# Router logits taken from raw rows and scaled after, expert rows gated on the way out of PSUM, last expert turn written out with column halves

## The reference, cut to what matters

```python
x = x + g_m * y                                     # end of the mixer
h = rms_norm(x, norm_ffn[l]) * (1.0 + sc_f) + sh_f  # 256 rows of 1024
logits = h @ w_router                               # 1024 -> 8
top_val, top_idx = lax.top_k(logits, 2)
top_w = jax.nn.softmax(top_val, -1)
for e in range(8):
    out = out + combine[..., e:e+1] * (silu(h @ w1[e]) * (h @ w3[e])) @ w2[e]
x = x + g_f * out
```

## Time and profile before

| what | value |
|---|---|
| median of 3 runs | 2612.45 us (2610.32 to 2614.62) |
| the profiled execution's own time | 2612.26 us |
| its span, first to last instruction | 2610.5 us |
| mean granted TensorE clock | 0.972 of 2.4 GHz |
| busy: PE, PEld, DVE, ACT | 2460.1, 1437.8, 614.0, 455.7 us |
| read from HBM | 583.14 MB |
| issue of the first expert load | 1676.29 us |

### The profile page before, as it was taken

How to read it: one execution, slowest core, us unless ns; L and a number is a source line. 1 busy time by engine, 2 the same in 40 slices (tenths; PEclk the granted TensorE clock), 3 DMA queues, 4 the chain that set the end, 5 groups by cost and what they waited for, 6 DMA issues and landing times.

```text
span 2610.5 us, 36347 instructions
## 1 busy us (share of the span) xinstructions
PE 2460.1 (94%) x15945; PEld 1437.8 (55%) x15945; DVE 614.0 (24%) x1457; ACT 455.7 (17%) x949; POOL 48.2 (2%) x67
## 2 busy tenths in 40 slices
PE   7999999999999999999999999799999889989987
PEld 5754776756685547777677655444443334333333
DVE  1241556713444320000144332300000001001001
ACT  1321123322213310000122142200010000001000
POOL 3300000000000000000000000000000000000000
PEclk9999899998999999999999999799999999999999
DMA  8633633327224137434532521399999999999995
GB/s 255 127 129 105 233 133 137 129 105 258 67 99 161 65 111 276 151 140 175 190 89 98 194 93 37 112 393 394 394 393 394 393 394 394 391 396 388 389 393 212
DMA packets 258237, 586.58 MB, mean 225 GB/s; under 512 B 14592, under 2 KB 16720, under 8 KB 258080
## 3 DMA queue, kind: packets, MB, share of 16 engines
q1 hardware_dynamic: 254304, 576.93, 60.2%
q0 software_dynamic: 3376, 5.94, 1.4%
q10 hardware_dynamic: 400, 1.36, 0.2%
HBM read 583.14 MB, written 1.06 MB: 224 GB/s over the span
## 4 chain that ended last, share of the span: by engine, by line
PE 84%; DMA 8%; SPq 3%; DVE 2%; ACT 1%; issue 1%; DVEq 1%; ACTq 0%
PE PSA L325 15%; PE PSB L2555 12%; PE PSA L340 10%; PE PSB L2489 7%; DMA RING<-in_w_moe 7%; PE PSA L2584 5%; PE PSA L2471 4%; PE PSB L2568 4%; PE PSA L699 3%; SPq L2847 3%; PE PSA L1278 2%; PE PSA L1901 2%; PE PSA L2594 2%; PE PSB L1470 1%; PE PSA L1852 1%
## 5 line engine op out<-in xcount | busy, mean ns | idle before, releaser
L2555 PE MATMUL PSB<-RING,Y 128*64 128x512 f32 x1792 | 399.9, 599 | 41.1 <-issue 20.8
L325 PE MATMUL PSA<-RING,HT 128*128 128x512 f32 (+1 forms) x896 | 392.5, 587 | 8.6 <-ACT Y L1441 5.0
L340 PE MATMUL PSA<-HT,RING 128*128 128x256 f32 x1216 | 277.8, 389 | 8.6 <-DMA RING<-in_w_in_ab 4.2
L2555 PEld LDWEIGHTS PSB<-RING,Y 128*64 128x64 f32 x1792 | 133.2, 138 | 270.4 <-issue 258.0
L325 PEld LDWEIGHTS PSA<-RING,HT 128*128 128x128 f32 x896 | 165.7, 191 | 183.2 <-issue 178.0
L340 PEld LDWEIGHTS PSA<-HT,RING 128*128 128x128 f32 x1216 | 235.0, 195 | 45.1 <-issue 11.7
L2584 PE MATMUL PSA<-RING,ROW 128*64 128x512 f32 x896 | 198.4, 595 | 5.6 <-issue 4.3
L2489 PE MATMUL PSB<-HT,RING 128*128 128x256 f32 x896 | 199.8, 381 | 2.0 <-DMA RING<-in_w_dense 2.0
L2489 PEld LDWEIGHTS PSB<-HT,RING 128*128 128x128 f32 x896 | 171.2, 191 | 37.2 <-issue 12.4
L2682 DVE TENSOR_TENSOR ROW<-ROW,PSB 128x512 f32<-128x512 f32 (+2 forms) x56 | 28.2, 504 | 589.7 <-PE PSB L2555 553.0
L2568 PE MATMUL PSB<-RING,Y 128*32 128x128 f32 (+1 forms) x3136 | 132.9, 289 | 0.0
(11 more groups left out here) (444 smaller groups left out, 2256.8 us busy)
## 6 DMA issues: line engine op xcount, KB each, us to landing
RING<-in_w_moe SPq DMA_DIRECT2D x168, 2048.0 KB, 20.1
RING<-in_w_ada SPq DMA_DIRECT2D x24, 2048.0 KB, 8.1
RING<-in_w_dense SPq DMA_DIRECT2D x21, 2048.0 KB, 11.9
RING<-in_w_in SPq DMA_DIRECT2D x20, 2048.0 KB, 11.6
RING<-in_w_in_c SPq DMA_DIRECT2D x15, 2048.0 KB, 8.0
RING<-in_w_in_ab SPq DMA_DIRECT2D x10, 2048.0 KB, 15.6
RING<-in_w_out SPq DMA_DIRECT2D x4, 2048.0 KB, 7.8
RING<-in_w_out_ab SPq DMA_DIRECT2D x3, 2048.0 KB, 7.8
```

Source lines behind the costliest of these rows:

```text
L325: mm = pe.matmul(PSA[:, lane[k], 512 * t:512 * t + cols], HT[:, c, P * t:P * t + P], W[:, c, 0:cols], start=(c == 0), stop=(c == KC - 1))
L340: mm = pe.matmul(PSA[:, lane[k], S * j:S * j + S], W[:, c, P * j:P * j + P], HT[:, c, :], start=(c == 0), stop=(c == KC - 1))
L2555: mm = pe.matmul((UP if up else GATE)[WIDE * which:WIDE * which + WIDE, :], HTG[:, c, WIDE * which:WIDE * which + WIDE], W[which][:, c, :] ...
```

## The change

- At the end of layer 1's mixer VectorE first runs `dve_moe_prepare`: scale, shift and gate of the second half of `mod`, `router_w` multiplied by the scale, the shift's product with the router's weights, the spreading of the gate, four memsets. Tile t=1 of the gated add is done in two column halves, each with its own `x_ready`.
- `pe_entry`, `act_entry`, `dve_entry` are not called for the experts. `pe_router` turns the raw rows of X (transposes), t=0 ahead of t=1; ScalarE copies three half tiles to HT and VectorE the fourth; the logits are `raw * rms + shift`, formed by VectorE after the root.
- `dve_router` goes through both tiles one after the other, signals `chosen`, and forms the rank as soon as the counts are there (two matmuls, ahead of the places); places, the first selection, weights and the count of turns come after `ranked`, in that order. The gate row is spread by eight matmuls behind the places. The phases "ffn", "experts done" and "ffn done" of layer 1 are gone; the slot numbers in the constants count from 1, which saves an offset.
- VectorE multiplies both OUT tiles by GATE_ROW as they go to YG; ACC starts as a copy of X (made in g=1 of turn 0).
- The loop runs over turns 1 and 2 and the last turn is written out, without its gathers. Its last two loads are four, by column halves, with two semaphores of their own; `down` of the last group runs half by half, as do the products with the gate, the scatters (order 0, 2, 1, 3), the adds and the store (four of 256 KB).
- In the first block some semaphores are merged, and GpSimd drains after its first memset instead of signalling `padded`.

The diff, cut to its core:

```diff
+            if l == 1:
+                dve_moe_prepare(dve)
             for t in range(NT):
...
-                dve.tensor_tensor(MIXED[:, t, :], PSA[:, t, :], GATE_ROW, ALU.mult)
-                dve.drain()
-                dve.tensor_tensor(X[:, t, :], X[:, t, :], MIXED[:, t, :], ALU.add).then_inc(sem("x_ready"), 1)
+                for cols in [slice(0, 512), slice(512, 1024)] if l and t else [slice(0, 1024)]:
+                    dve.tensor_tensor(MIXED[:, t, cols], PSA[:, t, cols], GATE_ROW[:, cols], ALU.mult)
+                    dve.drain()
+                    dve.tensor_tensor(X[:, t, cols], X[:, t, cols], MIXED[:, t, cols], ALU.add).then_inc(sem("x_ready"), 1)
...
         def pe_router(pe):
+            need(pe, "gate_spread")
+            for t in range(NT):
+                for hf in range(2):
+                    if t == 0 and hf == 0 or t == 1:
+                        need(pe, "x_ready")
+                    for c in range(4):
+                        mm = pe.transpose(PSB[:, 2 * t + hf, P * c:P * c + P], X[:, t, 512 * hf + P * c:512 * hf + P * c + P], ident)
+                    mm.then_inc(sem("h_turned"), 1)
+                if t == 0:
+                    pe.matmul(PSA[:, 0, N_EXP:2 * N_EXP], CF[:, C_ONE:C_ONE + P], router_shift, start=True, stop=True)
+                for c in range(KC):
...
+                    mm = pe.matmul(PSA[:, 0, 512 * t:512 * t + N_EXP], HT[:, c, P * t:P * t + P], router_w[:, c, :],
+                                   start=(c == 0), stop=(c == KC - 1))
+                mm.then_inc(sem("logits"), 1)
+            need(pe, "chosen")
+            for t in range(NT):
+                mm = pe.matmul(COUNTS, CF[:, C_ONE:C_ONE + P], chosen[:, t, :], start=(t == 0), stop=(t == NT - 1))
+            mm.then_inc(sem("places"), 1)
...
+            for c in range(KC):
+                mm = pe.matmul(PSB[:, c // 4, P * (c % 4):P * (c % 4) + P], SPREAD[:, c, :], ident, start=True, stop=True)
+            mm.then_inc(sem("gate_row"), 1)
...
         def act_router(act):
+            for t in range(NT):
+                need(act, "x_ready")
+                if t:
+                    need(act, "x_ready")
+                act.activation(H2[:, t, :], X[:, t, :], ACT.Square, accum_out=rms_x[:, t:t + 1])
+                if t:
+                    act.drain().then_inc(sem("x_squared"), 1)
+                for hf in range(2 - t):
+                    act.wait_ge(sem("h_turned"), H_TURNED + 2 * t + hf + 1)
+                    act.activation(HT[:, 4 * hf:4 * hf + 4, P * t:P * t + P], PSB[:, 2 * t + hf, :].rearrange("p (c q) -> p c q", c=4),
+                                   ACT.Copy).then_inc(sem("h_taken"), 1)
+            act_rs(act, rms_x)
...
         def dve_router(dve):
+            need(dve, "x_squared")
+            k = dve_rs_ask(dve, rms_x, 1.0 / D, EPS)
+            dve.wait_ge(sem("h_turned"), H_TURNED + 4)
+            dve.tensor_copy(HT[:, 4:8, P:2 * P], PSB[:, 3, :].rearrange("p (c q) -> p c q", c=4)).then_inc(sem("h_taken_late"), 1)
+            dve.wait_ge(sem("rs_done"), k)
+            for t in range(NT):
+                need(dve, "logits")
...
+                dve.scalar_tensor_tensor(logits[:, t, :], PSA[:, 0, 512 * t:512 * t + N_EXP], rms_x[:, t:t + 1], router_shift,
+                                         ALU.mult, ALU.add)
...
+            dve.drain().then_inc(sem("chosen"), 1)
+            dve.tensor_tensor(top_w[:, :, 1], top8[:, :, 1], top8[:, :, 0], ALU.subtract)
+            dve.drain().then_inc(sem("act_input"), 1)
+            need(dve, "places")
+            dve.scalar_tensor_tensor(rank_key, COUNTS, float(N_EXP), place, ALU.mult, ALU.subtract)
+            dve.drain()
+            dve.max(rank_sorted, rank_key)
+            dve.drain()
+            dve.max_index(rank_i.bitcast(U32), rank_sorted, rank_key)
+            dve.drain().then_inc(sem("ranked"), 1)
...
+            for hf in range(2):
+                pe.wait_ge(sem(f"last_columns{hf}"), 32)
+                down_wide(GROUPS - 1, (512 * hf,), False)
+                down_extra(GROUPS - 1, (512 * hf,)).then_inc(sem("last_rows"), 1)
+            pe.wait_ge(sem("misc_free"), pieces(turn, SCATTERS + 1))
+            for piece in LAST_PIECES:
+                pe.wait_ge(sem("moe_rows"), turn + (piece % 2 + 1))
+                scatter_piece(pe, piece, piece).then_inc(sem("last_rows"), 1)
...
-            act.wait_ge(sem("item_used"), used(turn, (0, "down", GROUPS - 1)))
-            act.activation(YG[0], OUT[0], ACT.Copy).then_inc(sem("moe_rows"), 1)
...
-            dve.tensor_copy(YG[1], OUT[1]).then_inc(sem("moe_rows"), 1)
...
+            if not end:
+                dve.wait_ge(sem("item_used"), used(turn, (0, "down", GROUPS - 1)))
+                for k in range(2):
+                    e = dve.tensor_tensor(YG[k], OUT[k], GATE_ROW, ALU.mult)
+                e.then_inc(sem("moe_rows"), 1)
+                return
+            for hf in range(2):
+                cols = slice(512 * hf, 512 * hf + 512)
+                need(dve, "last_rows")
+                for k in range(2):
+                    e = dve.tensor_tensor(YG[k][:, cols], OUT[k][:, cols], GATE_ROW[:, cols], ALU.mult)
+                e.then_inc(sem("moe_rows"), 1)
+            for piece in LAST_PIECES:
+                need(dve, "last_rows")
+                dve_add(dve, piece, piece).then_inc(sem("result"), 1)
...
+            for hf in range(2):
+                for j in (PER_TURN - 2, PER_TURN - 1):
...
+                    if hf == 0:
+                        sp.wait_ge(sem("item_used"), last * PER_TURN + (STATIC + j - SLOTS + 1))
+                    sp.dma_start(slot_view(j)[:, :, cols], src).then_inc(sem(f"last_columns{hf}"), 16)
```

More of the change, by code:

```diff
@@ L2325, in dve_router @@
-            for t in range(NT):
-                dve.tensor_scalar(chosen1, place, top8[:, t, 0:1], None, ALU.is_equal)
-                dve.drain()
-                dve.scalar_tensor_tensor(chosen[:, t, :], place, top8[:, t, 1:2], chosen1, ALU.is_equal, ALU.add)
+                dve.drain()
+                dve.tensor_copy(top_f[:, t, :], top_i[:, t, :].bitcast(U32))
+                dve.drain()
+                dve.tensor_scalar(chosen1, place, top_f[:, t, 0:1], None, ALU.is_equal)
+                dve.drain()
@@ L2329, in dve_router @@
+                dve.scalar_tensor_tensor(chosen[:, t, :], place, top_f[:, t, 1:2], chosen1, ALU.is_equal, ALU.add)
                 dve.drain()
             dve.drain().then_inc(sem("chosen"), 1)
-            need(dve, "top_exp")
+            dve.tensor_tensor(top_w[:, :, 1], top8[:, :, 1], top8[:, :, 0], ALU.subtract)
+            dve.drain().then_inc(sem("act_input"), 1)
+            need(dve, "places")
+            dve.scalar_tensor_tensor(rank_key, COUNTS, float(N_EXP), place, ALU.mult, ALU.subtract)
@@ new lines, in dve_router @@
+            dve.drain()
+            dve.max(rank_sorted, rank_key)
+            dve.drain()
+            dve.max_index(rank_i.bitcast(U32), rank_sorted, rank_key)
+            dve.drain().then_inc(sem("ranked"), 1)
+            dve.tensor_copy(rank_f, rank_i.bitcast(U32))
+            need(dve, "places")
+            for t in range(NT):
+                dve.scalar_tensor_tensor(e_place[:, t, :], PLACES[:, 8 * t:8 * t + 8], 1.0, chosen[:, t, :], ALU.add, ALU.mult)
+            dve.drain()
+            dve.tensor_tensor(PERMUTE, place.unsqueeze(1).broadcast_to([P, N_EXP, N_EXP]),
+                              rank_f.unsqueeze(2).broadcast_to([P, N_EXP, N_EXP]), ALU.is_equal)
@@ new lines, in dve_router, with by_rank @@
+            dve.drain()
+            halves = [slice(0, 4), slice(7, 3, -1)]
+            def by_rank(to, src):
+                for t in range(NT):
+                    dve.tensor_tensor(PERMUTED[:, t, :, :], PERMUTE, src[:, t, :].unsqueeze(1).broadcast_to([P, N_EXP, N_EXP]), ALU.mult)
+                dve.drain()
+                for which in range(2):
+                    dve.tensor_reduce(to[which][:, :, 0:4], PERMUTED[:, :, halves[which], :], AX.X, ALU.add)
+                dve.drain()
+            by_rank(t_place, e_place)
@@ L2332, in dve_router @@
+            dve_select(dve, 0)
+            dve.drain().then_inc(sem("select"), 1)
+            need(dve, "act_output")
             dve.tensor_scalar(top_w[:, :, 0], top_w[:, :, 1], 1.0, None, ALU.add)
@@ L2336, in dve_router @@
             dve.tensor_tensor(top_w[:, :, 1], top_w[:, :, 1], top_w[:, :, 0], ALU.mult)
-            for k in range(2):
-                dve.memset(t_weight[k], 0.0)
-                dve.memset(t_place[k], -1e9)
             dve.drain()
@@ L2626, in pe_moe_turn @@
                 turned(0, g)
-                if g == GROUPS - 1:
+                if g == GROUPS - 1 and not end:
                     misc(SCATTERS + 1)
@@ L2691, in dve_moe_turn @@
                     dve.drain().then_inc(sem("select_w"), 1)
-                if g == 1:
+                if g == 1 and not begun:
```

(8 more changed lines are left out.)

265 lines of the change are left out of this document (123 added, 142 removed).

## The result

The changed kernel takes **2586.45 us** (median; 2584.51 to 2592.07), the kernel before beside it 2610.32 (2604.19 to 2614.62), five runs each: ratio 0.9913, 95% interval 0.9893 to 0.9933. The forecast was 2590.0, range 2585 to 2599. The profiled execution took 2586.45 with a span of 2584.3. The medians measured side by side differ by 23.9; the forecast of 2590.0 was counted from 2612.26, and 1.9 of its 3.6 us of distance is that starting point, since the kernel before came out at 2610.32 here.

What follows compares the result with a forecast made beforehand. Expert loads were taken to pace the kernel, leaving gains only before the first issue and behind the last loads: 11.5 + 1.9 + 7.1 + 1.9 = 22.4 us off 2612.26, forecast 2590.0, range 2585 to 2599.

Steps and rivals of the forecast that it cites:

- Part 1: Router, from the mixer's last output product to the first expert load's issue: 11.5 us gained, bounds 9 and 12.5.
- The logits of the second tile: Router on PE: ready by 1658.7 at half clock, wanted at 1659.3, so hidden.
- The halves of the gated add: Ahead of the router: adding t=1 in two halves makes the last x_ready some 0.35 us later.
- The cover of the selection: Between rank and first expert product: PE starts 12.5 us behind the first issue, not 16; the feed hides later work.
- The stretch: Expert loads: 168 of 2 MB at 5.37 us each, about 902 us without a hole, pace unchanged.
- Part 2: Work behind the last loads: 1.9 us gained on PE, 7.1 in scatters and adds, 1.9 in the store.
- PE behind the loads: Last group's products without gathers: PE ends 1.9 us sooner, bounds 1.5 and 3.5.
- From there to the last add and the issue of the last piece: Behind the last down: 15.1 us become 8.0 (four scatters, one add, handovers), 7.1 gained.
- The store: End of kernel: last piece 0.26 MB instead of 1.05 MB, 1.9 us gained, bounds 0.5 and 2.0.
- The toll for each DMA: Rival, last loads and store: each DMA pays 1.8 us in turn, giving 2592.8 us; chance 0.10.
- Half the gain in the router's chain given back: Rival, router: rank only about 6 us earlier, 5.5 less gained, giving 2595.5 us; chance 0.10.
- PE as the bound in the last turn: Rival, written-out last turn: code fetching makes PE 15% slower, giving about 2620 us; chance 0.04.

Runs made afterwards that it cites:

- early_first_load: Changed kernel with root table loaded earlier, VectorE copying tile 1's first half, and first load issued after one register read: 2588.15 us.
- rank_behind_weights: Changed kernel with the rank signalled in the old order, behind exponential, weights and places: 2590.51 us.
- tile1_whole: Changed kernel with the gated add of tile 1 back at full width with one signal: 2590.24 us, one run.
- loads_in_two: Changed kernel with each 2 MB expert load (166 of them) split into two of 1 MB: 2594.86 us.
- one_store: Changed kernel with one 1 MB store behind the last add instead of four of 256 KB: 2593.6 us.
- filled_router: early_first_load plus full-width gated add of tile 1 and unused 128-column transposes between the logits products: 2587.92 us.
- select_: Two runs: changed kernel with six or seventeen extra VectorE memsets behind the rank signal, delaying selection: 2592.24 and 2615.66 us.

## Why the prediction was right

It was right in its terms as well as in its sum. **Part 1**, each step set against M: the issue was forecast 14.3 us behind it and came 14.28 behind. Shifted by the 3.0 by which M was earlier, the root ended at 1657.0 (forecast 1657.3), `chosen` was there at 1660.8 (1661.1), the rank's index at 1662.9 (1662.95). Two small errors cancelled, which is luck: the root came 0.3 sooner, since table load and root take 1.59 in the earlier trace rows themselves where 1.8 were counted, and from counts to index VectorE took 1.06 instead of 0.8. The logits of the second tile were said to be hidden with 0.6 to spare at half clock. In this profile they ended with 0.0 to spare, having taken 3.58 us where 16 records at 6 per us are 2.7: VectorE took up the second tile at 1656.04, the moment they were there. A little more gained before them and they would have been the bound in an execution like this one, as early_first_load shows; in six of the other eight profiles the same records were 0.4 to 1.15 us quicker, and where nothing else ahead of the issue was changed, I−M is the same to 0.1. rank_behind_weights measured 1.8 for the order of the signal, whose steps the forecast had not priced apart from the rest.

**The halves of the gated add** were priced at 0.35 lost; tile1_whole shows 0.45 lost.

**The cover of the selection.** The forecast said that PE gains 3.5 us on the feed and that the feed hides what comes behind. It gained 2.6 (13.35 against 15.99), and gave 1.6 of that back at once in a first product of 8.70 instead of 7.09. The remaining cover is 9.5 us; the sum did not depend on it.

**The stretch** stayed rigid, 883.8 us from first issue to last up pair in every kernel that didn't hold PE by more than 10.

**Part 2.** PE behind the loads: 2.3 us where 1.9 was forecast. The down pair of group 5 began 10.18 us after the up pair (forecast 10.7, before 11.12), so the landing was nearly 0.5 sooner than two loads of 5.37 make it; from its beginning to the end of the last down 18.36 us passed (18.3 forecast). From there to the last add and the issue of the last piece: 7.1 gained as forecast. The store: 2.2 in the profile, 2.0 when undone, 1.9 forecast. Forecast 22.4, measured 23.2 by stages and 23.9 between the medians; the other 2.7 of the distance from 2590.0 to 2586.45, of which 1.9 are the starting point, are of the size of the scatter ahead of M, so a hit within 3.6 us is in part luck. The bounds of the forecast's terms add up to 18.1 and 25.1, not to 17.5 and 25.3; the range of 2585 to 2599 holds either way.

**The rivals.** The toll for each DMA fell with loads_in_two and one_store: these DMAs did not pay it one after the other. Half the gain in the router's chain given back: fell, with 11.55 of 11.5. PE as the bound in the last turn: fell, since U−I, which holds all of that turn but its end, is 883.79 with and without the turn written out, and T−U is shorter. PE became the bound for a while only when it was held 36 us at the start.

## What to carry to other kernels

Where the DMA engines stand at a share of 1.04 from first byte to last, look for time only ahead of the first issue and behind the last landing, and work out each of these as a chain of its own. Cut the last transfer out so that only its last piece is waited for, and apply a factor to rows as they leave PSUM rather than in a pass behind the last product. Before shortening a chain further, ask which hidden branch has no slack left, and look at more than one execution: here the second tile's logits had none in one profile and over a microsecond in another, depending on when the clock fell.

## What was not expected of the hardware

- In the changed kernel the clock was 1.00 up to 1651 and then 0.50 until about 1664.5, as these windows show, though PE had been busy 16.9 of the 17 us up to 1651. Ahead of the fall it had run transposes and products of 8 columns; behind it came more of these, from 1660 on eight products of 128 columns, and then the gathers, during which the clock rose. The second tile's sixteen matmul records took 3.58 us where the first tile's took 1.95. In filled_router, with transposes of 128 columns between them, the clock stayed at 1.00 through both, even while PE waited for `chosen`. In six of nine profiles of the same code it fell 2 us later than in the other three.

```profile
1650.00:1651.00 1.00, 1.00 (x11) 1.00 (x11) 0.42 (x1) 0.49 (x1) 0.00 (x0) 1.00 0.00 0
1658.00:1660.00 2.00, 2.00 (x11) 2.00 (x11) 0.58 (x5) 0.20 (x1) 0.00 (x0) 0.50 0.00 0
1664.00:1664.50 0.50, 0.50 (x4) 0.50 (x3) 0.42 (x3) 0.50 (x1) 0.00 (x0) 0.50 1.01 373
```

- A delay that was meant as 5.5 us came out as 6.9: VectorE stands idle for 0.53 us between two of the memsets of 2048 columns, where 0.08 had been counted from the products of 1024 columns in the earlier trace rows. The idle time stands ahead of a memset rather than behind it. Behind the last of the three the next operation begins after 0.16, and the kernel before has the same 0.53 ahead of its one such memset, which follows operations of 8 columns:

```profile
1681.66 1.76 DVE L2392 MEMSET PROJ<- 128x2048 f32 x1 [0.53 <-issue]
```

- Executions of the same code differ by up to 16 us ahead of M and by 0.4 us from first load to last up pair (select_* left out): nearly all the scatter of these profiles lies where the kernel is not paced by the loads.
